# HGRN head: the masked scores of both directions are summed on VectorE and multiplied with the values once

## What is computed

```python
def hgrn_direction(q, k, v, log_f):
    ...
    def step(state, inp):
        qb, kb, vb, fb = inp
        b = jnp.cumsum(fb, axis=2)
        o_inter = jnp.einsum("bhtk,bhkv->bhtv", qb * jnp.exp(b), state)
        diff = b[:, :, :, None, :] - b[:, :, None, :, :]
        decay = jnp.exp(jnp.where(lower_tri, diff, -jnp.inf))
        scores = jnp.einsum("bhtk,bhsk,bhtsk->bhts", qb, kb, decay)
        o_intra = jnp.einsum("bhts,bhsv->bhtv", scores, vb)
        ...
        return new_state, o_inter + o_intra
...
    o_fwd = hgrn_direction(qh, k_f, vh, lf_f)
    flip = lambda t: jnp.flip(t, axis=2)
    o_bwd = flip(hgrn_direction(flip(qh), flip(k_b), flip(vh), flip(lf_b)))
    o = rms_norm(o_fwd + o_bwd, o_norm)
```

## Time and profile before

| | us |
|---|---|
| median of 3 runs | 2467.63 |
| lowest and highest run | 2464.0, 2469.48 |
| the profiled execution | 2469.33 |
| its span, first to last instruction | 2467.6 |

### The profile page before, as it was taken

The page is one execution under the profiler, slowest core; times in us unless marked ns, Lnnn a source line. Parts: engine busy times, 40 slices in busy tenths (PEclk is TensorE's granted clock), DMA queues, the critical chain, the costliest instruction groups (busy, mean ns, idle before and its releaser), DMA issues.

```text
span 2467.6 us, 37399 instructions
## 1 busy us (share of the span) xinstructions
PE 2344.5 (95%) x14290; PEld 2075.8 (84%) x14290; DVE 1580.9 (64%) x2311; ACT 1271.6 (52%) x1383; POOL 226.5 (9%) x53
## 2 busy tenths in 40 slices
PE   6999988999999999989899988977999999999999
PEld 6999977888888888878788867867888888888888
DVE  6777766677666676666566665654556555655566
ACT  6555554666666665445566675444344334433333
POOL 4777720000000000000000000000000000000000
PEclk9999999999999999999999988988999999999999
DMA  5444444444444443545444422531455555555556
GB/s 220 171 171 174 174 164 163 171 165 168 154 154 156 156 162 108 203 146 215 156 149 153 153 86 76 183 133 69 171 187 188 189 187 187 188 189 190 191 194 221
DMA packets 57426, 409.45 MB, mean 166 GB/s; under 512 B 6496, under 2 KB 6624, under 8 KB 8544
## 3 DMA queue, kind: packets, MB, share of 16 engines
q1 hardware_dynamic: 57312, 407.82, 45.4%
HBM read 405.70 MB, written 2.10 MB: 165 GB/s over the span
## 4 chain that ended last, share of the span: by engine, by line
PE 88%; ACT 4%; DVE 4%; issue 3%; DMA 1%; SPq 0%; DVEq 0%; ACTq 0%
PE G L347 23%; PE G L346 23%; PE G L345 11%; PE G L348 11%; PE G L354 4%; PE G L356 4%; PE G L355 4%; DMA RAW<-stream_dram 1%; ACT HI L323 1%; PE A L977 1%; DVE LO L330 1%; PE A L964 1%; PE A L1004 1%; DVE HN L454 0%; PE A L979 0%
## 5 line engine op out<-in xcount | busy, mean ns | idle before, releaser
L323 ACT ACTIVATE HI<-RAW 128x2048 fp32r<-128x2048 f32 x381 | 728.1, 1913 | 848.1 <-DMA RAW<-stream_dram 847.2
L330 DVE TENSOR_TENSOR LO<-RAW,HI 128x2048 fp32r<-128x2048 f32 x332 | 760.2, 2290 | 325.4 <-ACT HI L323 323.7
L347 PE MATMUL G<-HX,HI 128*128 128x512 f32 x2056 | 834.1, 406 | 44.6 <-DVE HX L473 20.7
L346 PE MATMUL G<-HX,HI 128*128 128x512 f32 x2056 | 819.9, 399 | 0.0
L345 PE MATMUL G<-HX,LO 128*128 128x256 f32 x2056 | 576.9, 281 | 0.0
L348 PE MATMUL G<-HX,LO 128*128 128x256 f32 x2056 | 575.2, 280 | 0.0
L345 PEld LDWEIGHTS G<-HX,LO 128*128 128x128 f32 x2056 | 390.6, 190 | 95.2
L348 PEld LDWEIGHTS G<-HX,LO 128*128 128x128 f32 x2056 | 392.0, 191 | 86.5
L347 PEld LDWEIGHTS G<-HX,HI 128*128 128x128 f32 x2056 | 395.5, 192 | 52.9 <-DVE HX L473 22.3
L346 PEld LDWEIGHTS G<-HX,HI 128*128 128x128 f32 x2056 | 389.8, 190 | 0.0
L337 POOL TENSOR_TENSOR LO<-RAW,HI 128x2048 fp32r<-128x2048 f32 x49 | 226.3, 4619 | 100.3 <-ACT HI L323 99.9
(11 more groups left out here) (347 smaller groups left out, 2559.0 us busy)
## 6 DMA issues: line engine op xcount, KB each, us to landing
RAW<-stream_dram SPq DMA_DIRECT2D x381, 1024.0 KB, 4.8
X<-x_dram SPq DMA_DIRECT2D x4, 512.0 KB, 5.2
MB<-mem_dram SPq DMA_DIRECT2D x4, 512.0 KB, 5.5
out_dram<-X SPq DMA_DIRECT2D x4, 512.0 KB, 7.7
CON<-constants_dram SPq DMA_DIRECT2D x1, 981.0 KB, 16.4
VEC<-vectors_dram SPq DMA_DIRECT2D x1, 623.5 KB, 17.4
VEC<-vectors_dram SPq DMA_DIRECT2D x1, 272.0 KB, 7.0
CON<-constants_dram SPq DMA_DIRECT2D x1, 64.5 KB, 1.9
```

The lines of the kernel that those rows point to most:

```text
L323: nc.scalar.activation(HI[:, c.slot(RING), :], RAW[:, c.slot(RING), :], ACT.Copy).then_inc(hi_ready, 1)
L330: nc.vector.tensor_tensor(LO[:, c.slot(RING), :], RAW[:, c.slot(RING), :], HI[:, c.slot(RING), :].bitcast(F32), ALU.subtract).then_inc(lo_ ...
L346: return nc.tensor.matmul(res, wh, both[:, k, :, :], start=False, stop=last)
L347: nc.tensor.matmul(res, wh, both[:, k, :, :], start=first, stop=False)
```

## The change

`output` drops the product that opened each half (L974). The first of the three state products of a half now carries the start flag, and the closing product takes SM[:, 0] in place of SM[:, 1]. On DVE a new step, `both_ways`, adds the backward masked scores onto the forward ones in place, 128 x 256 float32, behind `values` in every head. It waits for the mask and counts on the same semaphore `hg_sm`, which now rises by two a head, so the two waits of PE on it are rewritten: `output` waits for the sum, `turn` for both steps of the head before.

```diff
             def output(p):
-                wait(pe, hg_sm, p + 1)
+                wait(pe, hg_sm, p.times(2) + 2)
                 wait(pe, hg_st, p + 1)
                 wait(pe, hg_og, p)
                 for tt in range(2):
                     o = A[5][:, tt * P:(tt + 1) * P]
-                    nc.tensor.matmul(o, VT[:, tt, :], SM[:, 0, tt, :], start=True, stop=False)
-                    for d, s in [(d, s) for s in range(3) for d in range(2) if order(d, s + 1) // 2 == tt]:
+                    for n, (d, s) in enumerate([(d, s) for s in range(3) for d in range(2) if order(d, s + 1) // 2 == tt]):
                         c = order(d, s + 1)
-                        nc.tensor.matmul(A[5][:, c * CH:(c + 1) * CH], SP_[:, d, s, :],
-                                         QT[:, d, c * CH:(c + 1) * CH], start=False, stop=False)
-                    mm = nc.tensor.matmul(o, VT[:, tt, :], SM[:, 1, tt, :], start=False, stop=True)
+                        nc.tensor.matmul(A[5][:, c * CH:(c + 1) * CH], SP_[:, d, s, :], QT[:, d, c * CH:(c + 1) * CH],
+                                         start=(n == 0), stop=False)
+                    mm = nc.tensor.matmul(o, VT[:, tt, :], SM[:, 0, tt, :], start=False, stop=True)
                 mm.then_inc(hg_o, 1)
...
-                wait(pe, hg_sm, h)
+                wait(pe, hg_sm, h.times(2))
...
+            def both_ways(p):
+                wait(dve, hg_sm, p.times(2) + 1)
+                nc.vector.tensor_tensor(SM[:, 0], SM[:, 0], SM[:, 1], ALU.add).then_inc(hg_sm, 1)
...
                     mask(p)
                     values(p)
+                    both_ways(p)
...
             values(last)
+            both_ways(last)
             gate(last)
```

## The result

| | before | after |
|---|---|---|
| median us | 2467.61 (6 runs) | 2455.88 (6 runs) |
| lowest and highest | 2464.0, 2469.48 | 2453.64, 2457.54 |
| profiled execution | 2469.33, span 2467.6 | 2453.64, span 2451.8 |

The changed kernel takes 0.995 of the time before, 95% interval 0.994 to 0.996: 11.7 us less, where I had forecast 7.2. The direction was right, the size 4.5 us too small.

What follows compares the result with a forecast made beforehand. PE was taken to bound the HGRN mixer without a gap from the second head on. 6.6 us from 15 outputs plus 0.6 in the last head gave 7.2 off, 2460.4 us against the median, range 2456.0 to 2465.8.

Steps and rivals of the forecast that it cites:

- The dropped product: PE's `output`: two openers of 0.22 us gone per head, 0.44 us, over 15 heads 6.6 us.
- the bounds, 4.2 and 9.0: Lowest and highest gain in us over 15 outputs, by whether the 0.08 us hand-over stays or goes with the opener.
- the rival of the kept hand-over: In `output`, each hand-over keeps its 0.08 us, an opener gives only 0.14: 4.6 us gain, 2463.0; chance 0.12.
- The sum: VectorE's added step behind the values' copy: 0.42 us, at most 0.84, hidden in idle time, costing nothing.
- What is late next: Head's end: keys' transposes keep 0.77 us or more to spare, weights further off, so the gain stays PE's.
- taken back at the turn: Rival at a head's end: VectorE's keys become late, all 6.6 us go, 0.6 stays: 2467.0; chance 0.05.
- The last head: Last `output`, at clock 0.50: 0.86 us saved, worth 0.43 to 0.86 by when the clock returns; 0.6 taken.
- the one on the loop's turns: PE's two HGRN loop turns: gaps of 1.4 and 1.7 us that nothing in the trace releases.
- one rival: Late code: both loop-turn gaps grow to 7.0 us and the clock falls, 12.5 us slower, 2480.1; chance 0.05.
- the range: Whole kernel: 2457.7 to 2463.0 us from the unknown terms, widened for the medians' movement to 2456.0 to 2465.8.

Runs made afterwards that it cites:

- e4: The kernel before plus the VectorE sum and its waits, written to a tile nobody reads, no product dropped: 2467.05 us, ratio 1.0002.
- e3: The changed kernel without the VectorE sum, so only the opening products are dropped and the output is not the reference's: 2456.78 us, ratio 0.9966.
- e2: The changed kernel with 60 more already-met wait instructions at the start of PE's program: 2462.12 us, ratio 0.9983.
- e9: The kernel before with 174 already-met wait instructions ahead of the HGRN loop, spread over three idle stretches of PE: 2465.6 us, ratio 1.0.
- e1: The kernel before with 200 already-met wait instructions at the start of PE's program: 2476.58 us, ratio 1.0049, first matmul after 27.4 us instead of 13.6.
- e7: The changed kernel with 30 already-met wait instructions at the start of PE's program; no median given, heads over the loop's turns 34.56 and 34.75 us.
- e6: The changed kernel with 8 dummy products filling PE's idle time ahead of the last head's output: 2453.21 us, ratio 0.9937.
- e5: The changed kernel as it is, timed again beside the kernel before: 2457.16 against 2467.86 us, ratio 0.9955.
- e8: The changed kernel with 28 already-met wait instructions inside PE's loop body; no median given, heads over the loop's turns 35.46 and 35.20 us.
- e10: The changed kernel with 15 already-met wait instructions at the start of PE's program; no median given, heads over the loop's turns 34.36 us twice.

## Why the prediction was too small

**The dropped product** was right in mechanism and size: 0.44 us a head forecast, 0.45 measured, 6.75 against 6.6 in all. Charging start to start was right. Of the bounds, 4.2 and 9.0, neither mattered, and the rival of the kept hand-over is out: the half stands at 0.89.

**The sum** was right: 0.41 us, hidden in every head and in the last, shown by e4 and by the unchanged 32.73 of e3.

**What is late next** was right: nothing. The keys never came last in a plain head, so the gain was not taken back at the turn.

**The last head** was right in kind, and my 0.6 a little high. From its keys' transposes to the product of `sums` PE took 12.41 us before and 11.56 after, 0.85 less. But the clock came back 8.8 us after PE set in again in both, at 976.9 and at 965.6, not earlier by the work saved:

```profile
961.00:965.60 4.60, 4.51 (x14) 3.85 (x15) 0.97 (x3) 4.44 (x6) 0.00 (x0) 0.50 0.00 0
965.60:970.00 4.40, 4.40 (x26) 3.88 (x26) 4.02 (x4) 4.38 (x3) 0.00 (x0) 0.98 0.00 0
```

So what was saved at half speed was worth half. The last evictions of the output projection, before and after, begin 104.25 and 103.78 us after the last head's keys, which is 0.47 less:

```profile
1065.06 0.42 DVE L630 TENSOR_TENSOR X<-X,G 128x256 f32 x1 [1.99 <-PE G L346]
```

```profile
1053.31 0.42 DVE L630 TENSOR_TENSOR X<-X,G 128x256 f32 x1 [2.06 <-PE G L346]
```

That the clock took 8.8 us both times is luck of these two executions. In the nine other profiles with the idle 3.74 us it was back after 6.6 (e2, e3) to 9.8 us (e9). In e3, which gives PE the same products there as the changed kernel, it took 6.6, and keys to last eviction 102.71 us. The rule that I cited (the Trainium skill, TensorE: Matmul & The Clock Gate, Part 1) has it that a time of activity brings the clock back and not a number of matmuls. The traces agree that no number of matmuls does, but they show no fixed time either, and what the clock does here moves the time by more than the 0.4 us saved.

**The step that failed** is the one on the loop's turns. I named the two gaps, saw that nothing released them, and put them into the sum as a constant and into one rival as something that could only grow. That the body gets shorter I even wrote down, as an argument against growth. It was the way to a gain: moving and shortening the code by 24 and 28 instructions brought it down to where it need not be fetched again. That is 3.6 us that the sum lacked and the range did not allow for. A cost whose cause the trace does not show needs a bound at zero as well as one at its worst. With the two gaps of the earlier trace rows bounded so, the largest gain is 9.9 + 3.1 = 13.0 us, at 2454.6 against the median, and holds the result. The range has a slip as well: 2457.7 less 2 is 2455.7 and not 2456.0. The right figure would have held the median of 2455.88, but by luck, as no term of it stood for the turns. The code queue by stretch, read in the trace of the kernel before, could have told ahead of the run that the loop was being fetched in each turn, though not that its gaps could go.

In sum: 6.75 in the heads, 3.6 at the turns and 0.4 in the last head make 10.8 us, against 11.7 and 10.7 measured on two occasions. The two profiled spans differ by more, 15.8 us. About 11.5 of it is there when the next mixer's first matmuls start, at 1104.0 and 1092.5, and 0.9 of these was there at the first head's keys (459.44 and 458.51), before any output had run. The rest arises in stages that the change does not touch. I put it down to the spread between executions of one kernel, 4 to 9 us here; it was not followed further. That the turns are worth 3.6 us is read from the heads in the traces. The times agree with it only roughly: 4.2 in e1, 6 in e2, and 1.2 at most in e9.

## What to carry to other kernels

Price a dropped product by its start-to-start time in a PE queue without gaps, and a vector step by the idle time that ends in the wait behind it; both held to a few hundredths of a microsecond. Then look at what else an edit moves: in a long loop of one engine (here some 1700 PE instructions), a few dozen instructions, even ones far ahead of it, decided whether each turn waits 1.6 to 2.7 us for code. The count of fetched code packets in the loop's stretch, 18 or none here, says on which side a kernel lies. Moving the loop takes the gaps away, but whether it pays must be measured: neither move of the old kernel (e1, e9) was faster than before. Where PE must idle in front of short work, a few dummy products that keep the clock up can be worth more than work saved behind the idle time, here 3.8 us against 0.4.

## What had not been expected of the hardware

- A PE loop of 1706 instructions turned without any fetch of code, and the same loop 15 instructions further on was fetched whole, about 9 packets of 16 KB a turn, at 1.6 us a turn.
- PE idles ahead of the first head's keys. Full clock followed in the kernel before (2.2 us of idle time), e4 (1.9), e7 (2.5), the changed kernel (2.8), e6 (3.0), e1 and e5 (3.2 each). Half clock for a while, at a loss of some 1.6 us, followed in e3 (2.4), e9 (2.7), e8 (3.1) and e10 (3.2), and at a loss of 2.7 in e2 (4.8). So between 2.2 and 3.2 us the length of the idle time alone did not decide it. It may be one source of the few microseconds by which executions of one kernel differ, as may the 6.6 to 9.8 us that the clock took to come back in the last head; that was not tried.
